# Where a chain of transformer blocks computes its Ada tiles, issues its row swaps and prepares its S5 matrices

## What is computed

```python
def reference(...):
    x = first_block(...)     # layer 0: HGRN2 mixer, layer 1: NSA attention; each with a SwiGLU network
    return second_block(x, ...)  # layer 0: differential attention, layer 1: S5; each with a squared-ReLU network
```

```python
mods = jnp.einsum('bd,lde->lbe', c_act, ada_w) + ada_b[:, None, :]     # 4 parts of 3 * 1024 numbers
# in each layer of the first block
shift, scale, gate = jnp.split(mods[2 * layer + 1], 3, axis=-1)
x = x + gate * swiglu(modulate(x, norm_ffn[layer], shift, scale), ffn_w_in[layer], ffn_w_out[layer])
# second block, layer 0: half of each head's 64 rows is swapped with the other half (rope)
q = apply_rope_2(rms_norm_2(q, q_gain), cos, sin) * (HEAD_DIM ** -0.5)
k = apply_rope_2(rms_norm_2(k, k_gain), cos, sin)
# second block, layer 1
b_bar = ((a_bar - 1.0) / lam)[..., None] * b_mat
```

## Time and profile before

| | |
|---|---|
| median of 3 runs | 3257.51 us (3255.71 to 3260.61) |
| the profiled execution | 3260.06 us |
| its span, first to last instruction | 3258.20 us |
| TensorE busy | 2914.1 us, 89% |
| weight loads of TensorE (beside its matmuls) | 2351.5 us, 72% |
| VectorE busy | 1692.5 us, 52% |
| ScalarE busy | 1090.2 us, 33% |
| GpSimd busy | 57.2 us, 2% |
| mean granted clock of TensorE | 0.934 |
| loaded from HBM | 292.00 MB, 96 GB/s with what is written |

### The profile page before, as it was taken

How to read it: one execution, slowest core, us unless ns; L and a number is a source line. 1 busy time by engine, 2 the same in 40 slices (tenths; PEclk the granted TensorE clock), 3 DMA queues, 4 the chain that set the end, 5 groups by cost and what they waited for, 6 DMA issues and landing times.

```text
span 3258.2 us, 38782 instructions
## 1 busy us (share of the span) xinstructions
PE 2914.1 (89%) x14906; PEld 2351.5 (72%) x14906; DVE 1692.5 (52%) x2444; ACT 1090.2 (33%) x1540; POOL 57.2 (2%) x42
## 2 busy tenths in 40 slices
PE   3999989999886789899999998798999875989998
PEld 2798768887674467778787776577887655778787
DVE  5566565655542556543333446748677373443342
ACT  2312333222322434433222444633232333343231
POOL 1003000000000000000000000000000000000000
PEclk7999999999896789799999999999999987999999
DMA  5550344555433000013332332024434544123232
GB/s 184 166 157 1 106 136 131 163 142 142 151 117 119 1 1 1 1 53 99 100 91 84 100 101 68 1 68 103 147 136 155 209 115 91 52 85 96 90 103 65
DMA packets 448551, 320.11 MB, mean 98 GB/s; under 512 B 14002, under 2 KB 435996, under 8 KB 448412
## 3 DMA queue, kind: packets, MB, share of 16 engines
q1 hardware_dynamic: 328592, 237.00, 25.1%
q10 hardware_dynamic: 119820, 81.18, 8.5%
HBM read 292.00 MB, written 19.86 MB: 96 GB/s over the span
## 4 chain that ended last, share of the span: by engine, by line
PE 73%; DVE 12%; ACT 4%; DMA 4%; issue 4%; ACTq 1%; POOL 1%; SPq 0%; DVEq 0%; POOLq 0%
PE ps L435 49%; PE ps L417 6%; PE ps L429 3%; PE ps L843 2%; DMA ada_ring<-in_ada_w 2%; DVE ada_ring L493 1%; DMA nsa_area<-nsa_area 1%; DVE ada_ring L1682 1%; PE ps L2533 1%; PE ps L829 1%; PE ps L816 1%; PE ps L1591 1%; PE ps L1556 1%; DVE ada_first L507 1%; DVE h_area L1686 1%
## 5 line engine op out<-in xcount | busy, mean ns | idle before, releaser
L435 PE MATMUL ps<-hh,whi 128*128 128x512 f32 x1744 | 690.6, 396 | 9.1 <-DVE wlo L389 4.8
L435 PE MATMUL ps<-hh,wlo 128*128 128x512 f32 x1744 | 681.4, 391 | 0.0
L435 PE MATMUL ps<-hl,whi 128*128 128x512 f32 x1744 | 680.9, 390 | 0.0
L389 DVE TENSOR_TENSOR wlo<-raw,whi 128x2048 fp32r<-128x2048 f32 x198 | 453.7, 2292 | 309.6 <-ACT whi L385 309.6
L385 ACT ACTIVATE whi<-raw 128x2048 fp32r<-128x2048 f32 x198 | 377.3, 1905 | 423.3 <-PE ps L435 255.9
L435 PEld LDWEIGHTS ps<-hh,whi 128*128 128x128 f32 x1744 | 329.0, 189 | 85.5 <-issue 11.1
L435 PEld LDWEIGHTS ps<-hl,whi 128*128 128x128 f32 x1744 | 329.0, 189 | 70.3 <-issue 3.1
L435 PEld LDWEIGHTS ps<-hh,wlo 128*128 128x128 f32 x1744 | 328.5, 188 | 68.8
L435 PE MATMUL ps<-hid_h,whi 128*128 128x512 f32 x756 | 306.2, 405 | 7.6 <-DVE wlo L389 7.6
L435 PE MATMUL ps<-hid_h,wlo 128*128 128x512 f32 x756 | 299.7, 396 | 0.0
L435 PE MATMUL ps<-hid_l,whi 128*128 128x512 f32 x756 | 299.5, 396 | 0.0
(11 more groups left out here) (397 smaller groups left out, 4311.5 us busy)
## 6 DMA issues: line engine op xcount, KB each, us to landing
raw<-in_ffn_w_in SPq DMA_DIRECT2D x44, 1024.0 KB, 6.0
ada_ring<-in_ada_w ACTq DMA_DIRECT2D x80, 512.0 KB, 4.0
raw<-in_ffn_w_up SPq DMA_DIRECT2D x32, 1024.0 KB, 5.3
raw<-in_ffn_w_down SPq DMA_DIRECT2D x32, 1024.0 KB, 5.8
raw<-in_ffn_w_out SPq DMA_DIRECT2D x32, 704.0 KB, 4.6
raw<-in_hgrn_w_in SPq DMA_DIRECT2D x16, 1024.0 KB, 6.0
raw<-in_attn_w_qkv SPq DMA_DIRECT2D x12, 1024.0 KB, 6.5
s_area<-cp_dram SPq DMA_DIRECT2D x6, 2048.0 KB, 10.4
```

The source lines that it names most:

```text
L389: nc.vector.tensor_tensor(wlo[:, par, :], raw[:, par, :], whi[:, par, :].bitcast(F32), ALU.subtract).then_inc(w_lo, 1)
L435: m = nc.tensor.matmul(ps[:, bank, :], tile(w, kt, j), x[:, kt, :], start=(kt == 0 and n == 0), stop=(kt == k - 1 and n == 2))
```

## The change

Four things. The Ada tiles of the first network: both `*_in` segments carry two tiles a block, part 2 in the first and part 3 in the second (22 tiles each, from tile 0), `ffn0_out1` none, and `n_q` one a block, tiles 20 to 23 of part 3. The row swaps: GpSimd's queue issues them instead of SyncE's, with two semaphores of their own, and those of block db also wait for the rotation of db − 2. S5: the last four of the six operations for `b_bar` go from hook 5 to hook 6, and the unit of hook 6 moves behind, so that hook 28 has two. Last, two semaphores of the output are shared with two of the start.

```diff
-        out_rdy, stored, out_ps = sem("out_rdy"), sem("stored"), sem("out_ps")
+        out_rdy, stored, out_ps = cols_rdy, sem("stored"), cols_ps
...
-                ada_in = ada_part(2, 11 * half, 1) if layer == 0 else None
-                ada = ((a["kv_ada_w"], 8, 104, 1), ada_part(3, 0, 2))[half] if layer == 0 else None
+                ada_in = ada_part(2 + half, 0, 2) if layer == 0 else None
+                ada = (a["kv_ada_w"], 8, 104, 1) if layer == 0 and half == 0 else None
...
-            add("n_q", 4, cols_of(a["nsa_w_q"][0], 0), 2, 0, ada=ada_part(3, 16, 2))
+            add("n_q", 4, cols_of(a["nsa_w_q"][0], 0), 2, 0, ada=ada_part(3, 20, 1))
...
-        turned_in = ((g_in, CMP_LOADS), (nsa_in, 80))
+        turned_in = ((sem("turned_even"), 0), (sem("turned_odd"), 0))
...
-        def d_turn(sp, db):
-
-            sp.wait_ge(ev_a, seg["d_q"].ea0 + 2 * db + 2)
-            if db >= 4:
-                sp.wait_ge(dn_rot, RP0 + 2 * db - 6)
+        def d_turn(pool, db):
+
+            pool.wait_ge(ev_a, seg["d_q"].ea0 + 2 * db + 2)
+            if db >= 2:
+                pool.wait_ge(dn_rot, RP0 + 2 * db - 2)
             slots = slice(2 * db % 8, 2 * db % 8 + 2)
             for row in range(0, P, 32):
-                sp.dma_start(d_rot[row:row + 32, slots, :], d_pair(db)[row ^ 32:(row ^ 32) + 32, :, :]
+                pool.dma_start(d_rot[row:row + 32, slots, :], d_pair(db)[row ^ 32:(row ^ 32) + 32, :, :]
                              ).then_inc(turned_in[db % 2][0], 16)
...
-        PER_BLOCK = [0] * 6 + [1, 1] + [1, 2, 1, 2, 1, 2, 1, 2] + [1] * 8 + [2, 1, 2, 1, 1, 1, 1, 1]
+        PER_BLOCK = [0] * 7 + [1] + [1, 2, 1, 2, 1, 2, 1, 2] + [1] * 8 + [2, 1, 2, 1, 2, 1, 1, 1]
...
             elif gb == 5:
-                tmp = tmp5.rearrange("p (h g) -> p h g", h=GH)
                 dve.wait_ge(s5_pp, 4)
                 tt(by_g(b_bar[:, 0, :, :]), taken(4), wide(wr), ALU.mult)
                 link(tt(by_g(b_bar[:, 1, :, :]), taken(4), wide(wi), ALU.mult))
+            elif gb == 6:
+                tmp = tmp5.rearrange("p (h g) -> p h g", h=GH)
                 dve.wait_ge(s5_pp, 5)
...
-                elif s.name in D0:
-                    for b in range(s.n):
-                        load(b, (s.g0 + b) % 2, True)
-                        if D0[s.name] + b >= 4:
-                            d_turn(sp, D0[s.name] + b - 4)
                 else:
                     each_block(sp, s, load)
...
             if upto >= 9:
+                for db in range(8):
+                    d_turn(pool, db)
                 diff_pool(pool)
```

More of the change, by code:

```diff
@@ L2008, in _ @@
                         load(b, (s.g0 + b) % 2, True)
-                elif s.name in D0:
-                    for b in range(s.n):
-                        load(b, (s.g0 + b) % 2, True)
-                        if D0[s.name] + b >= 4:
-                            d_turn(sp, D0[s.name] + b - 4)
                 else:
                     each_block(sp, s, load)
-            sp.wait_ge(out_rdy, 2 * TT)
+            sp.wait_ge(out_rdy, 2 * TT + 1)
             sp.dma_start(out[0].rearrange("(t p) d -> p t d", p=P), xin[:, :, :]).then_inc(stored, 16)
@@ L2495, in _ @@
             for n in range(2 * TT):
-                dve.wait_ge(out_ps, n + 1)
+                dve.wait_ge(out_ps, n + 3)
                 nc.vector.tensor_copy(xin[:, n // 2, n % 2 * T:(n % 2 + 1) * T], ps[:, n % 4, :]
@@ L2646, in _ @@
                 if n >= 4:
-                    pe.wait_ge(out_rdy, n - 3)
+                    pe.wait_ge(out_rdy, n - 2)
                 for i in range(4):
```

## The result

| | before | after |
|---|---|---|
| median | 3256.61 us (3253.11 to 3260.61, 4 runs) | 3216.57 us (3214.51 to 3223.23, 4 runs) |
| profiled execution, with its span | 3260.06 us, 3258.20 us | 3223.23 us, 3221.5 us |
| TensorE's share of the chain of waits | 73% | 76% |
| DMA's share of it | 4% | 2% |

The changed kernel takes 0.988 of the time before, 95% interval 0.9865 to 0.9895. The medians differ by 40.0 us, and the two profiled executions by 36.8. The forecast was 3215 us (3205 to 3235). It added up to -43.0 for the profiled pair, 6.2 us more than was measured there, so the parts have to be looked at one by one.

What follows compares the result with a forecast made beforehand. TensorE was taken as the bound (73% of the span), with only gaps between matmul blocks to win. Terms -16.8 - 18.7 - 7.5 = -43.0 took 3260.06 to 3217.1 us; against the median, 2.5 lower: 3215 us, range 3205 to 3235.

Steps and rivals of the forecast that it cites:

- the two short waits: TensorE waits of some 3 us ahead of `ffn0_out0`'s first block and about 3 us behind `mlp0_out0`'s first block.
- Part 1: Ada tiles moved out of `ffn0_out1` into `ffn0_in0` and `ffn0_in1`: -16.8 us (-13 to -19).
- The lag: `ffn0_in0`: Ada sums run 4.7 us behind TensorE after the first block's late load, shrinking to about 3 after eleven.
- I take +3: End of `ffn0_in0`: cost of TensorE waiting for the last Ada sums, +3 us (0 to 5).
- the new wait of part 3: Behind `mlp0_out0`'s first block TensorE waits 2.8 us for unit 0; a lower clock behind it may take up to 1.7.
- Part 2: Row-swap copies in `d_q` to `d_v` issued by GpSimd, so TensorE sets the pace: -18.7 us.
- The price of the copies: Four row-swap copies on GpSimd taken as on SyncE, 8.2 us until used; free up to 16.9 us.
- rival C: Row swaps: GpSimd's queue does four copies one after another, 33 us a turn; slower than before, 3373 us. Chance 0.05.
- Part 3: S5 input matrices around `mlp0_in0` and `mlp0_out0`: earlier `hid_f` lets block 9 start earlier, -7.5 us (-5.5 to -9).
- own bound of -46: Largest total gain in the bounds of the forecast's sum, -46 to -32 us, from which the range was drawn.
- A: `ffn0_in0` and `ffn0_in1`: Ada loop of 12.0 us, 0.6 over the matmuls, 22 times: +13 us, 3228. Chance 0.12.
- B: Row swaps: GpSimd's copies arrive late or weren't the cause, gain gone: +18.7 us, 3234. Chance 0.15.

Runs made afterwards that it cites:

- Early loads: Whole change, with the two Ada tiles of the first `ffn0_in0` block loaded ahead of the second norm: 3212.75 us, 0.9857 of the kernel before.
- another order: Whole change, but row-swap copies back on SyncE, ahead of the weight load of the block four turns on: 3220.69 us, 0.9880 of the kernel before.
- the copies one by one: Whole change, but GpSimd waits for each copy of a turn to land before issuing the next: 3223.04 us, 0.9888 of the kernel before.
- the kernel with a loop 0.5 longer than the block: Whole change plus one extra VectorE product in each block of `ffn0_in0` and `ffn0_in1`: 3235.53 us against 3220.49 for the whole change.
- the second part alone: Kernel before, with only the 32 row-swap copies issued by GpSimd instead of SyncE: 3241.72 us, 0.9940 of the kernel before.

## Why the prediction was right

**What bounds the kernel.** Right. The three places where the chain left TensorE are gone from it, and the two short waits that the forecast named are the only waits that came in where the change works.

**Part 1: -13.9 instead of -16.8.** The loads were worth what the forecast took: 99.46 - 76.35 = 23.1 us against 24.1. The 0.8 us by which the last two tiles' products stand behind `ffn0_in1` are in the 76.35. From the end of the first `ffn0_out0` block to `n_kvc` the forecast has -24.1 + 2.4 + 0.3 = -21.4 and the trace -21.0. The lag also came as worked out: `hid_f` at 467.91 (467.6 in the forecast), 4.4 us behind TensorE, 3.4 after eleven blocks (3), a turn of 11.23 us (11.0 to 11.2). Early loads removed it, as the mechanism says. The term that was mis-sized is "I take +3": the wait was 3.2 us and the block behind it 1.5 longer by the lower clock, 4.7 together, near the top of its bounds (0 to 5). The forecast allowed for exactly this behind the new wait of part 3, and left it out here. `n_q` gave 0.5 instead of 0.9.

**Part 2: -19.1 instead of -18.7.** `d_q` and `d_k` ran at 12.62; `d_v` at 11.51 where 11.65 was taken, four times, which is the rest. The choice of `h_v`'s row over the 12.9 at the lower clock was right: with no waits ahead, the clock stayed up (granted 1.00 from 1913.3 to 1961.0). The price of the copies was wrong and it didn't matter. I took SyncE's 8.2 us as a property of four copies, and put the rotation 9 to 14 us behind a block's end. It came at 1841.65, 5.8 us behind the end at 1835.85. What had made them 8.2 us was the 1 MB load ahead of them: with another order the same queue needs 4.15. For the same reason rival C's 33 us a turn was no real bound: strictly one by one, a turn took 10.0 to 14.0. The Trainium skill, "DMA: Bandwidth & Descriptors", section "Anatomy of one DMA", gives an estimated 2.3 us for one such copy. The trace of the copies one by one on GpSimd agrees, in the view of line 1047, where only those behind a load took much longer:

```profile
DMA to landing us min/median/max: 2.1/2.2/6.2
```

Four times the page's figure, as the forecast estimated, is not what happens when they are issued one right behind the other: they overlap and are used after 4.3 us.

**Part 3: -6.3 instead of -7.5.** The second block of `mlp0_out0` began 8.0 us earlier (119.31 to 111.27 us behind the start of `mlp0_in0`), between the forecast's 7.8 and 8.9, and the new wait was 2.86 (2.8). Of the 8.0 the lower clock took 0.86. Another 0.87 went to transposes. The forecast said of the moved unit that it "is VectorE work under a block with room"; but the units are dealt in order, so with one fewer at the front a unit with eight transposes on TensorE falls behind a block of `mlp0_in1` that had none (2387.49 in the chain of after). 8.04 - 0.86 - 0.87 = 6.3. That was the step overlooked.

**The sum.** The parts as measured in the traces make -39 (-43.0 in the forecast), and the medians differ by 40.0. The forecast's misses are +2.9, -0.4 and +1.2, and 0.3 for the later start; the largest single ones are the lower clock behind the wait in part 1 (1.5) and the transposes of part 3 (0.87). That the median came within 1.6 us of the 3215 is in part luck: the parts miss by 4.0, and by medians the same change gave 36.3 us (3260.33 to 3224.02) and 41.4 (3261.84 to 3220.49) in the two later comparisons. The low end of the range, 3205, doesn't follow from the forecast's own bound of -46 either, which gives 3257.5 - 46 = 3211.5.

**The rivals.** A (loop longer than the block) didn't come, but its price was fair: it gave 13 us for 0.6 us a block, and the kernel with a loop 0.5 longer than the block lost 15.0. B fell with the second part alone, -18.6. C fell with the changed kernel and with the copies one by one. The lock-out of descriptor writing that C named was hardly put to the test: of the 1.94 us in which GpSimd issued a turn, VectorE was at work, with `tensor_tensor`, for the last 0.4 or so (from 1838.90 in the turn of 1837.35).

## What to carry to other kernels

A small copy that stands behind a big load in a queue is issued as late as the load may be, and lands with it (here 6.1 us after its issue, the load 6.5 after its own). The first is what cost the time here, since it closed a loop; the length of a turn was hidden once the turn was issued in time. Before giving such a copy to another engine, look at what it stands behind, and issue it first. A wait that is left in front of TensorE costs more than its length: add the longer block behind it, 0.9 to 2.3 us for waits of 2.9 to 5.6 us here. And when work is moved to a block "with room", count it on each engine that it uses; the room is only on one of them.

## What the runs showed that I had not expected

- Four copies of 128 KB within the chip's SBUF took 4.15 us from the first issue on SyncE to their use and 4.3 on GpSimd. Behind a 1 MB load of the same queue it was 8.6. A single one was issued in 0.49 us on GpSimd and in 0.59 (median) on SyncE.
- The load of 1 MB also delays copies of another queue, though the load is SyncE's and the copy GpSimd's: 4.0 to 6.2 us passed behind the six copies issued up to 1.8 us after one, 2.2 to 3.3 behind the others.
- The cost of the lower clock isn't a fixed figure even at the same place, nor did it simply grow with the wait: the first block of `ffn0_out0` took 9.34 us behind a wait of 3.2 us and 10.10 behind 4.1 in two executions of the changed kernel, and 9.36 behind the 5.6 of the longer loop, instead of 7.80.
- The stretch from `d_v` to `mlp0_in0` took from 177.0 to 180.0 us in kernels with the same code there, the same to 0.03 us in each execution of one kernel that was profiled more than once, and with it went the granted clock in the attention loop (0.94 to 0.89). What selects it stays open.
